# Long convolution of a hybrid encoder layer: transforms at odd half frequencies with even and odd samples apart

## The reference, cut to what matters

```
def fft_long_conv(u, kern, skip):              # u [1, 256, 256], kern [512, 256]
    L = u.shape[1]
    U = jnp.fft.rfft(u, n=2 * L, axis=1)
    K = jnp.fft.rfft(kern, n=2 * L, axis=0)
    y = jnp.fft.irfft(U * K[None], n=2 * L, axis=1)[:, :L]
    return y + u * skip.astype(jnp.float32)

def hyena_mixer(...):
    u = centred_short_conv(u_proj, conv_w, conv_b)      # 3 taps
    v, x1, x2 = jnp.split(u, 3, axis=-1)
    kern = hyena_filters(L, ...)                # forward half, 0, backward half
    z = x1 * fft_long_conv(v, kern[:, 0], skip[0])
    y = x2 * fft_long_conv(z, kern[:, 1], skip[1])
    return rms_norm(y, out_norm)
```

## Time and profile before

| what | us |
|---|---|
| median of 3 runs | 1089.18 |
| lowest, highest | 1088.64, 1089.37 |
| span of the profiled execution, first to last instruction | 1087.3 |
| PE busy | 1053.6 |
| DVE busy | 587.2 |
| ACT busy | 493.3 |
| POOL busy | 103.5 |

### The profile page before, as it was taken

The page is one execution under the profiler, slowest core; times in us unless marked ns, Lnnn a source line. Parts: engine busy times, 40 slices in busy tenths (PEclk is TensorE's granted clock), DMA queues, the critical chain, the costliest instruction groups (busy, mean ns, idle before and its releaser), DMA issues.

```text
span 1087.3 us, 18211 instructions
## 1 busy us (share of the span) xinstructions
PE 1053.6 (97%) x7148; PEld 949.8 (87%) x7148; DVE 587.2 (54%) x630; ACT 493.3 (45%) x656; POOL 103.5 (10%) x165
## 2 busy tenths in 40 slices
PE   6999999999989999999989999999998999999996
PEld 6999999778768999999889999998796789999995
DVE  4644454755665654445465544457456655445544
ACT  6443344447434544443364344335555354433342
POOL 2000000330341000000010000005004210000000
PEclk9999999999979999999999999999999899999999
DMA  9565455253212455545545555554252126554551
GB/s 327 197 219 186 182 190 193 80 192 140 106 56 88 158 191 193 193 169 182 191 166 197 191 193 187 181 173 148 99 181 78 39 79 232 187 183 174 190 204 48
DMA packets 26277, 178.38 MB, mean 164 GB/s; under 512 B 3152, under 2 KB 3664, under 8 KB 5360
## 3 DMA queue, kind: packets, MB, share of 16 engines
q1 hardware_dynamic: 24912, 174.73, 44.3%
q0 software_dynamic: 880, 2.74, 0.8%
q10 hardware_dynamic: 432, 0.18, 0.1%
HBM read 176.94 MB, written 1.05 MB: 164 GB/s over the span
## 4 chain that ended last, share of the span: by engine, by line
PE 63%; issue 28%; POOL 5%; ACT 1%; DVE 1%; DMA 1%; POOLq 0%; DVEq 0%; SPq 0%; ACTq 0%
PE psum L882 20%; PE psum L883 20%; PE psum L884 20%; POOL mixer_scratch L306 3%; PE psum L1103 1%; PE psum L899 1%; DMA w_raw<-in_w_dram 1%; PE psum L972 1%; ACT w_high L367 1%; POOL statistics L283 1%; POOL mixer_scratch L333 0%; POOL mixer_scratch L338 0%; POOL statistics L293 0%; ACT mixer_scratch L438 0%; PE psum L967 0%
## 5 line engine op out<-in xcount | busy, mean ns | idle before, releaser
L588 DVE TENSOR_TENSOR w_low<-w_raw,w_high 128x2048 fp32r<-128x2048 f32 x163 | 375.3, 2305 | 245.7 <-ACT w_high L367 245.7
L882 PE MATMUL psum<-xT_high,w_high 128*128 128x256 f32 x1536 | 436.1, 284 | 5.4 <-DVE xT_low L593 4.5
L883 PE MATMUL psum<-xT_low,w_high 128*128 128x256 f32 x1536 | 434.6, 283 | 0.0
L884 PE MATMUL psum<-xT_high,w_low 128*128 128x256 f32 x1536 | 434.6, 283 | 0.0
L367 ACT ACTIVATE w_high<-w_raw 128x2048 fp32r<-128x2048 f32 x163 | 311.1, 1914 | 124.9 <-PE psum L884 119.9
L882 PEld LDWEIGHTS psum<-xT_high,w_high 128*128 128x128 f32 x1536 | 294.6, 192 | 8.9 <-DVE xT_low L593 5.3
L883 PEld LDWEIGHTS psum<-xT_low,w_high 128*128 128x128 f32 x1536 | 294.6, 192 | 1.5
L884 PEld LDWEIGHTS psum<-xT_high,w_low 128*128 128x128 f32 x1536 | 294.6, 192 | 0.0
L396 ACT ACTIVATE silu_gate<-psum 128x256 f32<-128x256 f32 x88 | 33.7, 383 | 273.1 <-PE psum L884 273.1
L882 PE MATMUL psum<-w_high,hT_high 128*128 128x512 f32 (+1 forms) x360 | 139.9, 389 | 0.0
L883 PE MATMUL psum<-w_low,hT_high 128*128 128x512 f32 (+1 forms) x360 | 139.7, 388 | 0.0
(11 more groups left out here) (163 smaller groups left out, 804.9 us busy)
## 6 DMA issues: line engine op xcount, KB each, us to landing
w_raw<-in_w_dram SPq DMA_DIRECT2D x163, 1024.0 KB, 4.8
x<-in_x_dram SPq DMA_DIRECT2D x2, 512.0 KB, 4.3
mixer_scratch<-in_fil_dram POOLq DMA_DIRECT2D x2, 512.0 KB, 6.8
out_dram<-x_normed SPq DMA_DIRECT2D x4, 256.0 KB, 2.1
mixer_scratch<-in_fil_dram POOLq DMA_DIRECT2D x2, 384.0 KB, 7.4
mixer_scratch<-in_fil_dram POOLq DMA_DIRECT2D x2, 352.0 KB, 5.9
dft<-in_dft_dram SPq DMA_DIRECT2D x1, 512.0 KB, 6.8
inverse_dft<-in_dft_dram SPq DMA_DIRECT2D x1, 512.0 KB, 6.5
```

Source lines behind the costliest of these rows:

```text
L588: e.tensor_tensor(WL[p][:], raw[p][:], WH[p][:].bitcast(F32), ALU.subtract).then_inc(s_lo.sem, 1)
L882: e.matmul(out, ah, bh, start=start, stop=False)
L883: e.matmul(out, ah, bl, start=False, stop=False)
L884: return e.matmul(out, al, bh, start=False, stop=stop)
```

## The change

The length-512 transform of the real sequence at the integer frequencies is replaced by one at odd half frequencies, (2f + 1) pi / 512 for f = 0 to 127 and their mirror images. The 256 samples are split into even and odd ones. The transform of each half over 128 frequencies is one product for the real and one for the imaginary part, with no sum over halves in PSUM; the spectrum at the lower frequencies is even + odd, at the mirrored ones even - odd. So a forward transform is four products where there were eight, the inverse four where there were eight, and the filters take four of 512 columns where there were ten. Neither DC nor Nyquist is special any more, so KB and the extra constants go.

To join the halves, ACT copies the odd one from PSUM to SBUF (filter_odd, spectrum_odd) and DVE adds and subtracts it (spectrum for the filters, the first two instructions of products for the sequence). products also does the whole complex product and joins the result for the inverse; it has eight instructions in place of five, with three waits of DVE on itself, and the two additions on POOL go. On PE the filter transforms move: the first pair between the two S_G2 slots, the second behind them; the gate products and the first turn_conv go between the two S_G1 slots. Positions are held in order of parity within the long convolution: turn_conv reads its tile with a stride of two, the filter's window and position features are permuted on the host, and the first group of the normed output is put back in order by strided writes of turned_high and turned_low.

```diff
-LINKS = {"dve": 24, "pool": 49, "act": 2, "pool_start": 4}
+LINKS = {"dve": 28, "pool": 49, "act": 2, "pool_start": 4}
...
-        dft = sb("dft", [P, T, 512])
-        idft = sb("inverse_dft", [P, 4, SEQ])
+        dft = sb("dft", [P, T, 256])
+        idft = sb("inverse_dft", [P, 4, P])
...
-        KB = sb("filter_nyquist", [P, 512])
...
+        ODD = TT.rearrange("p (a b) n -> p a (b n)", b=2)
...
+        def by_parity(v):
+
+            return v.rearrange("p (m t) -> p t m", t=T)
...
-                for rows_, a, b in ((HYF, F_Z, F_DFT), (P, F_WIN, F_Z), (P, F_DFT, F_SKIP), (1, F_SKIP, NFIL)):
+                for rows_, a, b in ((HYF, F_Z, F_SKIP), (P, F_WIN, F_Z), (1, F_SKIP, NFIL)):
...
-                e.wait_ge(h_pr.sem, h_pr.at(l, 1))
-                e.tensor_tensor(Y, Y, TT, ALU.add).then_inc(h_y.sem, 1)
                 e.wait_ge(a_qt.sem, a_qt.at(l))
                 e.tensor_tensor(xn[:, :, 768:1024], TT[:, 0:2, :], TT[:, 2:4, :], ALU.add).then_inc(a_qr.sem, 1)
                 levels(l, 0)
-                e.wait_ge(h_pr.sem, h_pr.at(l, 2))
-                e.tensor_tensor(Y, Y, TT, ALU.add).then_inc(h_y.sem, 1)
                 levels(l, 1)
                 levels(l, 2)
...
+            def filter_odd(l, part):
+                e.wait_ge(k_mm.sem, k_mm.at(l, 2 * part + 1))
+                copy(ODD[:, part], PS[:, 7, :], k_oc)
+
+            def spectrum_odd(l, o, bank):
+                e.wait_ge(h_u.sem, h_u.at(l, 2 * o + 1))
+                copy(ODD[:, 0], PS[:, bank, :], h_oc)
...
-                hi(l, S_G1); hi(l, S_G1 + 1)
+                hi(l, S_G1)
+                filter_odd(l, 0)
+                hi(l, S_G1 + 1)
...
+                filter_odd(l, 1)
...
-                for n, (dst, b) in enumerate(((KB[:], 4), (KA[:, 0, :], 2), (KA[:, 1, :], 3), (KI[:, 0, :], 0), (KI[:, 1, :], 1))):
-                    e.wait_ge(k_mm.sem, k_mm.at(l, n + 1))
-                    copy(dst, PS[:, b, :], k_ev)
-                natural(l, 1, 2, 7)
+                natural(l, 1, 2, 4)
...
+                spectrum_odd(l, 0, 1)
                 hi(l, S_UKV)
...
+                spectrum_odd(l, 1, 7)
                 hi(l, S_WO + 1)
...
+            def spectrum(l, part, dst):
+
+                e.wait_ge(k_mm.sem, k_mm.at(l, 2 * part + 2))
+                e.wait_ge(k_oc.sem, k_oc.at(l, part + 1))
+                odd = ODD[:, part]
+                e.tensor_tensor(dst[:, 0, :], PS[:, 4, :], odd, ALU.add)
+                e.tensor_tensor(dst[:, 1, :], PS[:, 4, :], odd, ALU.subtract).then_inc(k_ev.sem, 1)
+
             def products(l, o, b):
 
-                e.wait_ge(h_u.sem, h_u.at(l, o + 1))
+
+                e.wait_ge(h_u.sem, h_u.at(l, 2 * o + 2))
+                e.wait_ge(h_oc.sem, h_oc.at(l, o + 1))
                 if o:
                     e.wait_ge(h_inv.sem, h_inv.at(l, o))
-                c = slice(o * 256, (o + 1) * 256)
-                ur = PS[:, b, :].rearrange("p (m n) -> p m n", m=2)
-                ui = PS[:, b + 1, :].rearrange("p (m n) -> p m n", m=2)
-                e.tensor_tensor(Y[:, 0:2, :], ur, KA[:, :, c], ALU.mult)
-                e.scalar_tensor_tensor(out=TT[:, 0:2, :], in0=ui, scalar=-1.0, in1=KI[:, :, c], op0=ALU.mult, op1=ALU.mult)
-                e.tensor_tensor(Y[:, 2, :], ui[:, 0, :], KB[:, c], ALU.mult)
-                e.tensor_tensor(Y[:, 3, :], ui[:, 1, :], KA[:, 1, c], ALU.mult)
-                e.tensor_tensor(TT[:, 2:4, :], ur, KI[:, :, c], ALU.mult).then_inc(h_pr.sem, 1)
+                even, odd = PS[:, b, :].rearrange("p (c n) -> p c n", c=2), TT[:, 0:2, :]
+                e.tensor_tensor(C[:, 0:2, :], even, odd, ALU.add)
+                e.tensor_tensor(C[:, 2:4, :], even, odd, ALU.subtract).then_inc(h_pr.sem, 1)
+                e.wait_ge(h_pr.sem, h_pr.at(l, o + 1))
+
+                def both(k):
+                    return bass.AP(k.tensor, k.offset + o * 256, [k.ap[0], [512, 2], [0, 2], [1, 256]])
+
+                def four(v):
+                    return v.rearrange("p (j c) n -> p j c n", c=2)
+                u, yy, tt = four(C), four(Y), four(TT)
+                e.tensor_tensor(yy, u, both(KA[:]), ALU.mult)
+                link(l, e.tensor_tensor(tt, u, both(KI[:]), ALU.mult))
+                e.tensor_tensor(yy[:, :, 0, :], yy[:, :, 0, :], tt[:, :, 1, :], ALU.subtract)
+                link(l, e.tensor_tensor(yy[:, :, 1, :], yy[:, :, 1, :], tt[:, :, 0, :], ALU.add))
+                e.tensor_tensor(C[:, 0:2, :], Y[:, 0:2, :], Y[:, 2:4, :], ALU.add)
+                e.tensor_tensor(C[:, 2:4, :], Y[:, 0:2, :], Y[:, 2:4, :], ALU.subtract).then_inc(h_y.sem, 1)
...
+                spectrum(l, 0, KA)
                 taps(l, 1, 4, 0, 0); taps(l, 2, 5, 1, 1)
...
+                spectrum(l, 1, KI)
                 lo(l, S_G1 + 1)
...
-                for part in range(2):
-                    for m in range(2):
-                        for p in range(T):
-                            r = e.matmul(PS[:, b + part, m * 256:(m + 1) * 256], dft[:, p, part * 256 + m * P:part * 256 + (m + 1) * P],
-                                         NV[:, 0, p, :], start=(p == 0), stop=(p == T - 1))
-                r.then_inc(h_u.sem, 1)
+                for p in (1, 0):
+                    for part in range(2):
+                        r = e.matmul(PS[:, b + p, part * 256:(part + 1) * 256], dft[:, p, part * P:(part + 1) * P], NV[:, 0, p, :], start=True, stop=True)
+                    r.then_inc(h_u.sem, 1)
+
+            def filter_dft(l, part):
+                for p in (1, 0):
+                    e.matmul(PS[:, (4, 7)[p], :], dft[:, p, part * P:(part + 1) * P], (HS, HD)[part][:, p, :],
+                             start=True, stop=True).then_inc(k_mm.sem, 1)
 
             def hy_inverse(l, o, b, halves=range(T)):
                 e.wait_ge(h_y.sem, h_y.at(l, o + 1))
                 for t in halves:
-                    for m in range(4):
-                        r = e.matmul(PS[:, b, t * 256:(t + 1) * 256], idft[:, m, t * P:(t + 1) * P], Y[:, m, :], start=(m == 0), stop=(m == 3))
+                    for part in range(2):
+                        r = e.matmul(PS[:, b, t * 256:(t + 1) * 256], idft[:, 2 * t + part, :], C[:, 2 * t + part, :], start=(part == 0), stop=(part == 1))
...
-                        r = e.transpose(PS[:, bank, t * 256 + j * P:t * 256 + (j + 1) * P], C[:, dst + j, t * P:(t + 1) * P], ident)
+                        r = e.transpose(PS[:, bank, t * 256 + j * P:t * 256 + (j + 1) * P], by_parity(C[:, dst + j, :])[:, t, :], ident)
...
-                for i in range(2):
-                    columns(l, 1, S_G2 + i, i, [(128 * n, n) for n in range(4)]).then_inc(s_used.sem, 1)
+                columns(l, 1, S_G2, 0, [(128 * n, n) for n in range(4)]).then_inc(s_used.sem, 1)
+                e.wait_ge(f_hs.sem, f_hs.at(l))
+                filter_dft(l, 0)
+                columns(l, 1, S_G2 + 1, 1, [(128 * n, n) for n in range(4)]).then_inc(s_used.sem, 1)
+                e.wait_ge(k_ev.sem, k_ev.at(l, 1))
+                filter_dft(l, 1)
 
                 e.wait_ge(q_n.sem, q_n.at(l))
                 e.wait_ge(q_kr.sem, q_kr.at(l))
@@ -1088,36 +1134,24 @@
                     r = e.transpose(PS[:, 6, SEQ + t * P:SEQ + (t + 1) * P], xn[:, t, 640:768], ident)
                 r.then_inc(q_tr.sem, 1)
 
-                e.wait_ge(s_fil.sem, s_fil.at(l, 64))
-                e.wait_ge(f_hs.sem, f_hs.at(l))
-                for b, what in ((4, 256), (2, None), (3, None), (0, 0), (1, P)):
-                    if b == 2:
-                        e.wait_ge(g_qk.sem, g_qk.at(l))
-                    if b == 0:
-                        e.wait_ge(c_conv.sem, c_conv.at(l, 2))
-                    for p in range(T):
-                        if what is None:
-                            w, h = dft[:, p, (b - 2) * P:(b - 1) * P], HS
-                        else:
-                            w, h = fil[:, F_DFT + p * 384 + what:F_DFT + p * 384 + what + P], HS if b == 4 else HD
-                        r = e.matmul(PS[:, b, :], w, h[:, p, :], start=(p == 0), stop=(p == T - 1))
-                    r.then_inc(k_mm.sem, 1)
-                    if b == 4:
-                        e.wait_ge(g_in.sem, g_in.at(l))
-                        for d in range(2):
-                            r = e.matmul(PS[:, 7, d * SEQ:(d + 1) * SEQ], wg[64:96, d, :], hid[64:96, 0, :], start=True, stop=True)
-                        r.then_inc(g_z.sem, 1)
-                e.wait_ge(g_az.sem, g_az.at(l))
-                turn_conv(l, 0, 7)
-                e.wait_ge(k_ev.sem, k_ev.at(l, 5))
-                for i in range(2):
-                    columns(l, 1, S_G1 + i, i, [(128 * n, n) for n in range(4)]).then_inc(s_used.sem, 1)
+                e.wait_ge(g_qk.sem, g_qk.at(l))
+                e.wait_ge(c_conv.sem, c_conv.at(l, 2))
+                columns(l, 1, S_G1, 0, [(128 * n, n) for n in range(4)]).then_inc(s_used.sem, 1)
+                e.wait_ge(s_fil.sem, s_fil.at(l, 48))
```

(10 more changed lines are left out.)

56 lines of the change are left out of this document (26 added, 30 removed).

## The result

The changed kernel takes 1090.93 us (median of 17 runs, 1089.33 to 1092.9), the kernel before 1089.38 beside it: a ratio of 1.0016, 95% interval [1.0009, 1.0022]. Forecast was 1085.9. The time lies inside the range, but in the case that I had given 0.22: no difference by the bound of 0.2%. What there is of one, 1.7 us, goes to the slower side, where a gain was forecast, and the interval lies above 1 as a whole.

What follows compares the result with a forecast made beforehand. PE, busy 97% of the span, was taken to bound the kernel, with waits for ACT and DVE taking back most of the saving. 1089.2 - 5.1 (gain) + 1.8 (clock) = 1085.9 us; range 1081.5 to 1092.9.

Steps and rivals of the forecast that it cites:

- the case that I had given 0.22: Rival of no difference, 1087.0 to 1091.4 us: the new gaps each bring a short low-clock spell; chance 0.22.
- Step 1: Layer 1 filters: ten products become four, net 5.7 us; PE would end S_G1 at 251.4 instead of 257.1.
- Step 2: Layer 1 S_G4: PE waits some 3.4 us for the taps; first transform starts at 266.3 against 269.06, 2.75 us gained.
- Step 4: Before the first inverse: DVE's eight product instructions take 6.2 us, the spectrum is ready at 278.4.
- The second gap: PE waits 3.2 us for DVE's products before the first inverse, which ends at 280.2 against 283.13.
- Step 6: Second products: DVE ends at 290.3, PE waits 0.8 us; the row maximum starts at 290.3 instead of 292.72.
- the third gap: PE waits 3.5 us before the scores of level 1, in place of the 1.07 us before 298.92.
- the charge for the clock: 0.9 us per layer for a low-clock spell started earlier or added by the third gap; between nothing and 2.5.
- the one long spell: PE at 1.2 GHz in the kernel before: about 305.0 to 318.7 in layer 1, 841.0 to 851.2 in layer 2.
- My own sign for the slower rival: Low clock inside 278 to 296 us would make the slower rival right.
- the slower rival: Clock falls in the second gap, about 278.5, and stays low: 1092.9 to 1103 us, from about 10 us on; chance 0.18.
- the net gain at full clock: Of 12.5 us less PE work per layer, 2.5 us reach the stage's end, 5.1 us in two layers.

Runs made afterwards that it cites:

- short_join: The changed kernel without the product with the imaginary part of the filters' spectrum and the two operations joining it; 1076.95 us, ratio 0.9881 to the kernel before.
- reorder: The changed kernel with ACT's weight split and DVE's short-convolution taps moved ahead of the gate's work, without fillers; 1084.09 us, ratio 0.9945 to the kernel before.
- half_products: The kernel before with half of the products of every transform left out and nothing added; 1077.89 us, ratio 0.9893 to the kernel before.
- fill_all: The changed kernel with useless PE products (fillers) in all its waits; 1084.46 us, ratio 0.9944 to the kernel before.
- fill_before: The kernel before with 8 fillers ahead of the scores of level 1 and 9 ahead of the Hyena output's transposes; 1085.69 us, ratio 0.9963.
- fill_first: The changed kernel with fillers in the first gap alone, the waits for the taps; 1090.2 us, ratio 1.0006 to the kernel before.
- early_half: The reordered changed kernel with fillers in the later gaps, spectrum semaphore raised after sum and difference, fewer fillers ahead of the inverse; 1077.86 us, ratio 0.9892.

## Why the prediction was wrong

**Right: the three gaps and where they stand.** Step 1, the turn at 245.0 and S_G1's end at 251.4, came at 245.54 and 251.87. Step 2's gap of 3.4 us came as 1.73 + 1.01, released by the taps, with a transpose between. Step 4's 6.2 us of products came as 6.33 (274.38 to 280.71); two 1024-wide ones start 1.14 us apart, the figure taken. The 6.6 us of the page's rule (the Trainium skill, VectorE: DVE Perf Modes, "The DRAIN you can't avoid") are farther off: 512-wide neighbours start 0.60 to 0.61 us apart and last 0.68. The prediction had used only half of what that section says; it adds that a next operation that is not held starts earlier. The rows fit that: ahead of the three instructions for which DVE waits on itself the distance is a whole duration (0.71 to 0.72 us behind a 512-wide one), elsewhere it is shorter. The second gap, 3.2 us, came as 3.11. Step 6's wait of 0.8 us came as 1.63, and the third gap of 3.5 as 1.50, because low clock stretched the work in front of it; without that it is the longer one (2.65 us in short_join, 3.09 in reorder). That much of the saving would be lost in waits for the other engines was right, and half_products shows it without the change; POOL's additions and the clock have a part in it there.

**Wrong first: the charge for the clock.** I charged 0.9 us per layer, all of it behind the row maximum, on the assumption that the third gap alone would move or lengthen the one long spell, and that its half-speed work would lie "mostly inside idle time". fill_all and fill_before put it at 1.9 per layer (3.8 in two, give or take 2). The step that failed is the count of low stretches: every new gap brought one of its own, the first two in dense work on the path, and the long one stayed (10.2 us in either layer, where layer 1 had 13.7). The profiled executions show it directly: ahead of the maximum, where I had charged nothing, the kernel after is 2.5 us behind fill_all in layer 1 (294.02 against 291.50). The rows of before that I used against it, PE half idle at 11.5 to 15.0 with the clock up, held for a different stretch and said nothing on these. I had this case as a rival ("the new gaps each bring a short low spell"), with the right price of up to 1.75 us for the second gap, and gave it 0.22. The page's warning (the Trainium skill, TensorE: Matmul & The Clock Gate, "HAM oscillation — how this bites in real kernels"), that waits between groups of products throw the clock back again and again, agrees with the trace: four low stretches in each layer where there was one. I should have moved the forecast by it. My own sign for the slower rival, low clock inside 278 to 296, did appear (from 281.2 and 294.9), but it can't tell that rival from this one.

**Wrong second: the net gain at full clock.** 2.5 us per layer were forecast, 5.1 in all; with the clock held it is 2.1 by the ratios, give or take 2. In layer 1 the maximum stands at 291.50 in fill_all, where I had 290.3, against 292.78 in fill_before: 1.3 us of 2.4. Each link was a little late: the transform 266.92 for 266.3 (ACT's split of the last S_G4 weight starts at 253.03 in the kernel after, some 0.7 later than worked out), the inverse 279.24 for 278.4, the products 6.33 for 6.2, twice. Ahead of the second products, DVE's level product and S_WO split last 0.93 and 2.60 us in fill_all where the kernel before has 0.68 and 2.49; POOL's sums of the level exponents run beside them, but that they are the cause is not shown. From the maximum to the end of the mixer the two kernels are alike in layer 1 (53.7 and 53.8 us to the first update of x, at 345.20 and 346.57). Layer 2 has the maximum of fill_all, then of fill_before, on DVE's timeline:

```profile
824.28 1.22 DVE L719 TENSOR_REDUCE statistics<-psum 128x4 f32<-128x1024 f32 x1
```
```profile
826.92 1.22 DVE L700 TENSOR_REDUCE statistics<-psum 128x4 f32<-128x1024 f32 x1 [2.22 <-PE psum L1036]
```

They are 2.64 us apart; 1.37 of it comes over from layer 1, so this layer gains another 1.3. From there to the first update of x fill_all takes 53.7 us and fill_before 52.2, and only fill_all has a low stretch there, of 3.4 us from 849.7. So the schedule gains 1.3 us per layer, 2.6 in all, half of what was forecast, and the 1.1 us between the spans has a low stretch in it that the fillers did not prevent.

Relative to the forecast ratio, 0.9970, the measured 1.0016 is 5.0 us off: 2.0 are clock and 3.0 gain. That the two add up is no test, since the gain was worked out from the same ratios. The slower rival (one spell of 10 us or more from the second gap) did not come in this kernel, but stretches of 20.5 us did, from the third gap of fill_first in layer 2 and of reorder in layer 1.

**Open.** What makes a low stretch last 3.4 us in one place and 20.5 in another was not settled, nor why one kernel has them in some runs and not in others (reorder). Fillers were tried in one amount for each gap but for early_half; a smaller dose might do.

## What to carry to other kernels

Work taken off a busy TensorE is worth what the next engine's chain leaves of it: follow ACT's and DVE's queues to the next point where PE needs them before counting products, and move the chain ahead together with the saving (the reordering gave 4 to 6 us behind this change and took 3 without it). Then count the gaps that the saving opens: charge each that stands ahead of dense work what a low stretch costs there (here 2.5 us for the two ahead of the maximum), and compare against the kernel before with its own clock losses removed. A kernel with such waits can be measured, and run, with useless products in them; that gave 4 us before the change and 8 behind it.

## What was not expected of the hardware

- PE that does more, and useless, work makes the program faster: 17 more products per layer take 4.0 us off the kernel before, 91 take 7.8 off the changed one, at mean clocks of 0.996 and 0.995 against 0.987 and 0.978.
- After the second gap the clock is still full as PE resumes and falls in the work behind it (1.00 in 278 to 280 with PE idle all of it, 0.81 in the next 2 us, 0.50 in those after). Elsewhere it fell inside the wait: at 260.8 in the kernel after, at 295.3 in reorder. In either case most of the low stretch, and so the price, lies behind the gap.
- In a stretch with gaps, half clock uses up the idle time that could have hidden it: with fillers PE is busy 8.25 of 12 us at full clock (306 to 318 in fill_before), without them 11.97 at half.
- Filling one gap of several gave 1.1 us on the changed kernel, not clear of noise (1.0006 [0.9997, 1.0016]); filling all gave 7.8 us.
- One and the same program, reorder, ran in 1077.18 us at a mean clock of 0.995 and in 1086.91 at 0.976.
